# HGRN projections by seven block products: 12 of 16 row tiles of 28 pairs of weight tiles, with the weight sums on GpSimd

## The chip, the cores and the metric

The kernel runs on one core of a Trainium2 chip. The metric is the device time of one execution in microseconds (us), of which the median of several runs is given. TensorE is called PE here, its weight loads PEld, VectorE DVE, ScalarE ACT, GpSimd POOL, and the queue that starts most transfers SP.

## The reference, cut to what matters

Two layers are computed for 512 prompt tokens and 32 sample tokens (T = 544 columns): RWKV-7, then HGRN2. Everything is float32. The change is in the second layer:

```python
q, f_logit, i, z = jnp.split(x @ w_in, 4, axis=-1)       # x: (544, 2048), w_in: (2048, 8192)
f = lb + (1.0 - lb) * jax.nn.sigmoid(f_logit)
k = (1.0 - lb) * jax.nn.sigmoid(-f_logit)
q = jax.nn.silu(q) * HGRN_DK ** -0.5
...                                                      # per head: decays, scores A, states S, output o
o = o * lax.rsqrt(jnp.mean(o * o, axis=-1, keepdims=True) + NORM_EPS) * norm_w
out = (o.reshape(B, T, D) * jax.nn.silu(z)) @ w_o
```

There are 16 heads of 128 columns, so each head needs four output tiles of 128 columns of `x @ w_in`, each summed over 2048 rows of weights, in 16 row tiles of 128.

## The kernel before

Channels lie on the 128 partitions and the 544 tokens along the free dimension. One weight tile is 128x2048: 16 row tiles (kt = 0 to 15) for 128 output channels. A float32 product is made of three faster ones: ACT rounds the tile (`split_hi`, line 1757, into `w_hi`), DVE subtracts to get the rest (`split_lo`, line 1972, into `w_lo`), and `x` is split in the same way into `x_hi` and `x_lo`. For each row tile PE then does `w_hi*x_hi`, `w_hi*x_lo` and `w_lo*x_hi`, each for both halves of the tokens (TH = 272 columns): six matmuls a row tile, 96 a weight tile (`dense_kt`, line 129).

The tiles are numbered g: 0 to 15 are the output projection of the first layer, H0 = 16 to H1 - 1 = 79 the HGRN projections (four a head, in the order f, q, v, z), 80 to 95 the last projection. PE goes through them in order and accumulates even tiles in the two banks of `pair[0]`, odd ones in those of `pair[1]`. Weights are loaded by SP into `raw[g % 2]` (1 MB), once ACT and DVE have split the tile that lay there.

Into PE's stream of the projections of head e small matmuls are put by hand (`dense(g, steps)`), after a certain row tile: eight score levels (`level`), the transposes `v_by_token` and `k_by_token`, the state update `kv`, and of the head before it `late(e - 1)`: `outputs`, `sample_out`, `sample_state`, `norm`. ACT, DVE and POOL have their own hand-written order for each head:

- When tile f is done, DVE scales it by the token's norm (`scaled_out`, line 2036) into `F`; ACT makes both sigmoids (`sigmoids`, lines 1820 and 1821); DVE applies the bounds (`gate`).
- When tile q is done, DVE scales it into `qr`, ACT applies silu (line 1824), DVE multiplies by F (`first_q`). `level(e, 0)` needs the silu and the gated K, `level(e, 1)` the product, and `level(e, n)` from 2 on needs what `widen(e, n - 2)` on DVE made of K and Q.
- `out_copy`, `head_root` (two logarithms, an exponential, each kind with its own table load) and on DVE `finish` normalize and gate the output row of the head before, in place in `o`.
- POOL has two operations a head: `Sd = Ss * decay` (line 1957) and `Vm` (line 1962).

Between the layers, DVE and ACT make the 16 normalized rows of `x` one by one (`normed`, `high_part`, `low_part`), and PE runs tiles 16 and 17 together behind them (`two_dense`). Then tiles 18 and on follow as `dense`.

## Time and profile before

| | |
|---|---|
| runs | 2890.67, 2893.17, 2893.42 us; median 2893.17 us |
| profiled execution | span 2890.2 us from the first to the last instruction; no time of its own is listed |
| PE busy | 96% of the span |
| DVE, ACT, POOL busy | 46%, 39%, 4% |
| mean granted clock of PE | 0.988 of full speed |
| tiles 16 to 79 | from about 1656 us to about 2680 us |

The span is shorter than the median by 3.0 us, which lies outside the first and the last instruction. In the rows below, times without a unit are us from the start of the span, and the value behind `|` is the sum in us and the mean in ns of one.

### The profile page before, as it was taken

What the parts mean: (1) busy time and instruction counts of PE and PEld (TensorE: products, weight loads), DVE (VectorE), ACT (ScalarE), POOL (GpSimd) and SP (SyncE); (2) the same over time, 40 slices, a digit from 0 to 9 for tenths busy, and PEclk for the clock granted to TensorE, in tenths of its full rate; (3) what the DMA queues carried; (4) which work ended last, traced back from release to release, by engine and by line L of the source; (5) the groups of instructions that cost most, each with busy time, mean ns of one, the idle gap of its engine ahead of it and who ended that gap; (6) DMA issues with size and microseconds to landing.
All of it is one profiled execution on the core that took longest, in us unless ns stands there. A gap on an engine that the chain in (4) does not pass through costs nothing.

```text
span 2890.2 us, 81902 instructions
## 1 busy us (share of the span) xinstructions
PE 2779.4 (96%) x37320; PEld 2623.6 (91%) x37320; DVE 1337.4 (46%) x2213; ACT 1137.5 (39%) x1559; POOL 108.1 (4%) x92
## 2 busy tenths in 40 slices
PE   6999999999999999999889899999999999999997
PEld 5899999999998888887789889999999999999997
DVE  7334313313327778887632364344443434444324
ACT  5344323324415555555432353343333343234322
POOL 0000000000001111111000000000000000000000
PEclk8999999999999999999999999999999999999999
DMA  3333333334211111112132242223222222222323
GB/s 124 110 105 108 111 111 111 111 111 145 103 69 48 53 53 53 53 53 78 31 130 88 81 144 75 97 75 98 90 89 75 97 75 98 90 90 75 128 88 107
DMA packets 79639, 262.29 MB, mean 91 GB/s; under 512 B 15936, under 2 KB 25920, under 8 KB 58816
## 3 DMA queue, kind: packets, MB, share of 16 engines
q1 hardware_dynamic: 70080, 239.23, 24.6%
q10 hardware_dynamic: 9216, 17.83, 1.6%
q8 instruction: 295, 4.83, 0.7%
q14 instruction: 48, 0.39, 0.0%
HBM read 216.06 MB, written 40.97 MB: 89 GB/s over the span
## 4 chain that ended last, share of the span: by engine, by line
PE 48%; ACT 1%; DVE 1%; issue 0%; DVEq 0%; ACTq 0%
PE t_pair L129 40%; PE t_lev L1603 1%; PE t_tok L1666 1%; PE t_pair L139 1%; PE t_lev L1677 1%; PE t_tok L1684 1%; PE t_tok L1644 0%; PE t_lev L1654 0%; PE t_tok L1559 0%; PE t_lev L1656 0%; PE t_lev L1616 0%; PE t_tok L1627 0%; PE t_tok L1636 0%; DVE keep_o L2186 0%; PE t_lev L1611 0%
## 5 line engine op out<-in xcount | busy, mean ns | idle before, releaser
L129 PE MATMUL t_pair<-t_x_hi,keep_w_hi 128*128 128x272 f32 x3008 | 658.8, 300 | 17.9 <-DVE t_x_lo L1999 9.6
L129 PE MATMUL t_pair<-t_x_lo,keep_w_hi 128*128 128x272 f32 x3008 | 622.9, 288 | 0.0
L129 PE MATMUL t_pair<-t_x_hi,keep_w_lo 128*128 128x272 f32 x3008 | 622.2, 288 | 0.0
L129 PEld LDWEIGHTS t_pair<-t_x_hi,keep_w_hi 128*128 128x128 f32 x3008 | 468.8, 189 | 48.3 <-issue 25.9
L129 PEld LDWEIGHTS t_pair<-t_x_lo,keep_w_hi 128*128 128x128 f32 x3008 | 474.7, 189 | 0.0
L129 PEld LDWEIGHTS t_pair<-t_x_hi,keep_w_lo 128*128 128x128 f32 x3008 | 471.4, 188 | 0.0
L129 PE MATMUL w_pair<-a_x_hi,keep_w_hi 128*128 128x272 f32 x2016 | 428.0, 294 | 19.8 <-DVE a_x_lo L1052 19.0
L129 PE MATMUL w_pair<-a_x_lo,keep_w_hi 128*128 128x272 f32 x2016 | 419.1, 289 | 0.0
L129 PE MATMUL w_pair<-a_x_hi,keep_w_lo 128*128 128x272 f32 x2016 | 416.8, 288 | 0.0
L1038 DVE TENSOR_TENSOR keep_w_lo<-keep_raw,keep_w_hi 128x2048 fp32r<-128x2048 f32 x63 | 144.4, 2292 | 470.1 <-ACT keep_w_hi L791 470.1
L129 PEld LDWEIGHTS w_pair<-a_x_hi,keep_w_hi 128*128 128x128 f32 x2016 | 319.8, 189 | 26.4 <-issue 21.4
L129 PEld LDWEIGHTS w_pair<-a_x_lo,keep_w_hi 128*128 128x128 f32 x2016 | 317.4, 189 | 0.0
L129 PEld LDWEIGHTS w_pair<-a_x_hi,keep_w_lo 128*128 128x128 f32 x2016 | 317.3, 189 | 0.0
L1972 DVE TENSOR_TENSOR keep_w_lo<-keep_raw,keep_w_hi 128x2048 fp32r<-128x2048 f32 x94 | 215.5, 2293 | 218.2 <-ACT keep_w_hi L1757 218.2
L1757 ACT CAST keep_w_hi<-keep_raw 128x2048 fp32r<-128x2048 f32 x94 | 178.4, 1898 | 194.6 <-PE t_pair L129 194.6
L805 ACT ACTIVATE a_stage<-w_pair 128x544 f32<-128x544 f32 x64 | 40.0, 625 | 425.1 <-PE w_pair L129 425.1
L791 ACT CAST keep_w_hi<-keep_raw 128x2048 fp32r<-128x2048 f32 x63 | 120.2, 1908 | 31.0 <-ACT a_stage L805 28.0
L426 PEld LDWEIGHTS w_pair<-b_Ti,b_MT 64*64 64x64 f32 x2560 | 80.9, 135 | 29.1 <-DVE b_Ti L1073 28.2
L426 PE MATMUL w_pair<-b_Ti,b_MT 64*64 64x64 f32 x2560 | 91.5, 221 | 16.5 <-DVE b_Ti L1073 14.6
L2076 DVE TENSOR_TENSOR t_K<-t_K,t_E 128x256 f32<-128x256 f32 (+1 forms) x96 | 41.0, 427 | 139.3 <-PE t_lev L1603 52.4
L426 PE MATMUL w_pair<-b_TiT,b_X 64*64 64x64 f32 x2560 | 93.0, 222 | 0.9 <-issue 0.9
L426 PEld LDWEIGHTS w_pair<-b_TiT,b_X 64*64 64x64 f32 x2560 | 82.0, 136 | 10.3 <-DVE b_X L1062 5.3
(363 smaller groups left out, 3793.0 us busy)
## 6 DMA issues: line engine op xcount, KB each, us to landing
keep_raw<-in_w_in SPq DMA_DIRECT2D x64, 1024.0 KB, 4.9
keep_raw<-in_hgrn_in SPq DMA_DIRECT2D x64, 1024.0 KB, 4.9
keep_raw<-in_rwkv_wo SPq DMA_DIRECT2D x16, 1024.0 KB, 4.9
keep_raw<-in_hgrn_wo SPq DMA_DIRECT2D x16, 1024.0 KB, 4.9
t_Ss<-in_hgrn_s SPq DMA_DIRECT2D x16, 512.0 KB, 4.4
out_hgrn_s<-t_Sd SPq DMA_DIRECT2D x16, 512.0 KB, 6.8
scr_r<-a_stage ACTq DMA_DIRECT2D x16, 272.0 KB, 2.1
scr_k<-a_stage ACTq DMA_DIRECT2D x16, 272.0 KB, 2.1
```

The lines of the kernel that those rows point to most:

```text
L129: mm = pe.matmul(out[:, a, 0:TH], w, x[:, kt, a * TH:(a + 1) * TH], start=(kt == 0 and n == 0), stop=(kt == KT - 1 and n == 2))
L139: mm = pe.matmul(out, w, x[:, kt, cols], start=(kt == 0 and n == 0), stop=(kt == KT - 1 and n == 2))
L426: return pe.matmul(out[rows(o_half)], lhsT[rows(i_half)], rhs[rows(i_half)], start=start, stop=stop, skip_group_check=not (start and stop))
L791: act.copy(w_hi[2 if n == 2 else n % 2][:, :], raw[n % 2][:, :]).then_inc(p.raw_hi, 1)
L805: act.activation(halves(stage[n % 2][:, :]), pair[3 if n == 2 else n % 2][:, :, 0:TH], func).then_inc(p.evac, 1)
L1038: dve.tensor_tensor(w_lo[b][:, :], raw[n % 2][:, :], w_hi[b][:, :].bitcast(F32), ALU.subtract).then_inc(p.raw_lo, 1)
L1603: mm = pe.matmul(out[32 * q:32 * q + 32, 32 * c:32 * c + 32], K[:, cols], rhs[:, cols], start=True, stop=True)
L1666: mm = pe.matmul(sm_ps[:, DS * b:DS * b + DS], Ss[:, b, :], Q[:, SEQ + DS * b:SEQ + DS * b + DS], start=False, stop=(b == NB - 1), skip_gr ...
L1677: pe.matmul(out[:, :], ktok[r, 4, :], Vm[r, :, :].rearrange("p b v -> p (b v)"), start=True, stop=True).then_inc(s.sn_mm, 1)
L1757: act.copy(w_hi[g % 2][:, :], raw[g % 2][:, :]).then_inc(s.raw_hi, 1)
L1972: dve.tensor_tensor(w_lo[g % 2][:, :], raw[g % 2][:, :], w_hi[g % 2][:, :].bitcast(F32), ALU.subtract).then_inc(s.raw_lo, 1)
L2076: dve.tensor_tensor(kp[:, :, 0, :], kp[:, :, 0, :], ep[:, :, 1:2].broadcast_to([P, nb, m]), ALU.mult).then_inc(s.kx, 1)
```

## The change

The four tiles of each head from 1 to 14 are taken in two pairs: (f, q) and (v, z). This gives NQ = 28 pairs, q = 0 to 27. In a pair the 12 row tiles from 0 to 11 are done as a product of 2x2 blocks: two output tiles, row tiles even and odd, tokens of the first and the second half. Seven block products (`product(0)` to `product(6)`) of six steps, three matmuls a step, take the place of eight. Row tiles 12 to 15 are done plainly (`rest`, 16 steps). A pair has 58 steps, which is 174 matmuls of 272 columns, where two tiles had 192. Heads 0 and 15 keep their four plain tiles.

- **Weights.** The products need four sums of weight blocks (128x768); POOL makes them (`weight_sum_1` to `weight_sum_4`) from both raw tiles of the pair. Each of the seven operands is rounded by ACT (`item_hi`) and subtracted by DVE (`item_lo`) in pieces of 768 columns, in three slots that take turns; the plain rest of each tile in pieces of 512 (`rest_hi`, `rest_lo`).
- **Rows of x.** Sums of rows are made once, between tile 17 and tile 19: ACT scales twelve rows again (`scaled_rows`), DVE makes four sums for each pair of rows (`row_sums`), and both split them (`sums_hi`, `sums_lo`). They lie where `o` was, so they begin when all rows of `x1` are written to HBM. Six more sums take the place of parts of `x_hi` and `x_lo` behind tile 19 (`third_sum_hi`, `third_sum_lo`); what stood there goes to HBM and back (b12).
- **Results.** The blocks are put together from four banks: ACT copies a bank out (`first_out`, `second_out`, `third_out`), DVE adds the next (`upper_first`, `upper_fifth`, `upper_second`, `lower_second`, `lower_first`).
- **Gated rows** of heads 0 to 13 no longer fit in `o`: they are made in `acc`, written to HBM, and read back behind the last pair.
- Tile 76 (the first of head 15) is done with its even row tiles last.

The diff, cut to what the prediction speaks of:

```diff
+U = 6
+UW = U * P
+CW = D - 2 * UW
+ITEMS = 7
+KT_ORDER = [*range(0, 2 * U, 2), *range(1, 2 * U, 2), *range(2 * U, KT)]
+KT_PLACE = [KT_ORDER.index(kt) for kt in range(KT)]
...
+        To = Area(nc, "u6", keep.o_at).sb("To", [P, KT, 2, TH], F32R)
+        Tl = Area(nc, "u7", keep.lora_at).sb("Tl", [P, 2, 2, TH], F32R)
...
+        def item_slot(q, k):
+            return slot[3] if (q, k) == (NQ - 1, ITEMS - 1) else slot[(ITEMS * q + k) % 3]
+
+        def item_source(k):
+            return (raw[0][:, 0:UW], raw[0][:, UW:2 * UW], S2[:, :], S1[:, :], S3[:, :], S2[:, :], raw[1][:, UW:2 * UW])[k]
...
+            def next_weights(q):
+                for sem in (s.it_hi, s.it_lo):
+                    sp.wait_ge(sem, ITEMS * q + 2)
+                for sem in (s.c_hi, s.c_lo):
+                    sp.wait_ge(sem, 2 * q + 1)
+                for sem in (s.s2, s.s3, s.s4):
+                    sp.wait_ge(sem, q + 1)
+                sp.dma_start(raw[0][:, :], weight_tile(GS + 2 * q + 2)).then_inc(raw_in[0], 16)
+                for sem in (s.it_hi, s.it_lo):
+                    sp.wait_ge(sem, ITEMS * q + ITEMS)
+                for sem in (s.c_hi, s.c_lo):
+                    sp.wait_ge(sem, 2 * q + 2)
+                sp.wait_ge(s.s1, q + 1)
+                sp.dma_start(raw[1][:, :], weight_tile(GS + 2 * q + 3)).then_inc(raw_in[1], 16)
...
+            sp.wait_ge(s.hi, 2 * KT)
+            sp.wait_ge(s.lo, 2 * KT)
+            for n, t in enumerate((x_hi, x_lo)):
+                sp.dma_start(b12_kept(n), b12(t)).then_inc(s.b12_out, 16)
...
+            for e in range(1, KT - 1):
+                next_weights(2 * e - 2)
+                sp.wait_ge(s.sd, e)
+                sp.wait_ge(s.so_mm, e)
...
+                states(e - 1)
+                sp.wait_ge(s.yz, e)
+                sp.dma_start(d.yz[e - 1], acc[:, :]).then_inc(s.y_spill, 16)
+                next_weights(2 * e - 1)
...
+            sp.wait_ge(s.used, ITEMS * NQ)
+            sp.wait_ge(s.y_spill, 16 * SPILLED)
+            for e in range(SPILLED):
+                sp.dma_start(o[:, e, :], d.yz[e]).then_inc(s.y_back, 16)
+            weights(GE + 2)
...
+            def seven_products(q, steps):
+                X, Y, V = (banks[(q + i) % 3] for i in range(3))
...
+                def three_passes(out, hi, lo, n, x, start):
+                    w = slice(n * P, n * P + P)
+                    for m, (a, b) in enumerate(((hi[:, w], x[0]), (hi[:, w], x[1]), (lo[:, w], x[0]))):
+                        mm = pe.matmul(out, a, b, start=start and m == 0, stop=(m == 2), skip_group_check=True)
...
+                    if m in steps:
+                        steps[m]()
+
+                def product(k, out, start):
+                    pe.wait_ge(s.it_hi, ITEMS * q + k + 1)
+                    pe.wait_ge(s.it_lo, ITEMS * q + k + 1)
+                    hi, lo = item_slot(q, k)
+                    for j in range(U):
...
+                if q == 0:
+                    pe.wait_ge(s.evac, GS - 1)
+                    pe.wait_ge(s.t_lo, 2 * U)
+                else:
+                    pe.wait_ge(s.f0, q)
+                product(0, X, True)
+                if q:
+                    pe.wait_ge(s.g1, q)
+                product(1, Y, True)
+                pe.wait_ge(s.c_hi, 2 * q + 1)
+                pe.wait_ge(s.c_lo, 2 * q + 1)
+                rest(0, 0, Y, False, None)
+                if q == 0:
+                    pe.wait_ge(s.evac, GS)
+                else:
+                    pe.wait_ge(s.c12, q)
+                rest(0, 1, Z, True, s.c_used)
+                pe.wait_ge(s.p1, q + 1)
+                product(2, X, False)
...
+                product(4, X, False)
+                product(5, Z, False)
+                pe.wait_ge(s.c_hi, 2 * q + 2)
+                pe.wait_ge(s.c_lo, 2 * q + 2)
+                pe.wait_ge(s.up, q + 1)
+                rest(1, 1, V, False, s.v_ready)
+                pe.wait_ge(s.u3, q + 1)
+                product(6, X, False)
+                rest(1, 0, X, False, s.c_used)
...
+                keys = [lambda: k_by_token(e - 1), lambda: kv(e - 1)]
+                if 1 <= e < KT - 1:
+                    steps = dict(zip((10, 13, 15, 17, 19, 21, 24, 27), late(e - 1)))
+                    if e > 1:
+                        steps.update(zip((2, 6), keys))
...
+            def scaled_rows(j):
...
+            def sums_hi(j):
+                even, odd = ((K, Q), (v, zs))[j % 2]
+                act.wait_ge(s.t_sum, 4 * j + 4)
+                act.copy(T1[j][:, 0], even[:, half(0)]).then_inc(s.t_hi, 1)
+                act.copy(T42[j][:, :, 0], halves(odd[:, :])).then_inc(s.t_hi, 1)
+
+            def third_sum_hi(j):
+                act.wait_ge(s.b12_used, j + 1)
...
 
             def out_tile(q, g, post):
                 m = g % KT
...
+                out_copy(e - 1)
+                second_out(q, F)
+                item_hi(q, 5)
+                head_root(e - 1)
+                item_hi(q, 6)
+                rest_hi(q + 1, 0)
+                act.wait_ge(s.lev_mm, NLV * (e - 1) + 1)
+                third_out(q, qr)
+                item_hi(q + 1, 0)
+                sigmoids(e)
+                item_hi(q + 1, 1)
...
+                    for j in range(U - 2, U):
+                        scaled_rows(j)
+                        sums_hi(j - 1)
+                    sums_hi(U - 1)
...
+            def weight_sum_1(q):
+                pool.wait_ge(raw_in[1], 16 * ((GS + 2 * q) // 2))
+                if q:
+                    pool.wait_ge(s.it_hi, ITEMS * (q - 1) + 4)
+                    pool.wait_ge(s.it_lo, ITEMS * (q - 1) + 4)
+                pool.tensor_tensor(S1[:, :], raw[1][:, 0:UW], raw[1][:, UW:2 * UW], ALU.add).then_inc(s.s1, 1)
+
+            def weight_sum_2(q):
+                pool.wait_ge(raw_in[0], 16 * ((GS + 2 * q) // 2))
+                pool.wait_ge(s.s1, q + 1)
+                if q:
+                    pool.wait_ge(s.it_hi, ITEMS * (q - 1) + 6)
+                    pool.wait_ge(s.it_lo, ITEMS * (q - 1) + 6)
+                else:
+                    pool.wait_ge(s.tile_ready, GS)
+                pool.tensor_tensor(S2[:, :], S1[:, :], raw[0][:, 0:UW], ALU.subtract).then_inc(s.s2, 1)
+
+            def weight_sum_3(q):
+                if q:
+                    pool.wait_ge(s.it_hi, ITEMS * (q - 1) + 5)
+                    pool.wait_ge(s.it_lo, ITEMS * (q - 1) + 5)
+                pool.tensor_tensor(S3[:, :], raw[0][:, 0:UW], raw[1][:, 0:UW], ALU.subtract).then_inc(s.s3, 1)
...
+            def item_lo(q, k):
+                hi, lo = item_slot(q, k)
+                dve.wait_ge(s.it_hi, ITEMS * q + k + 1)
+                dve.tensor_tensor(lo[:, :], item_source(k), hi[:, :].bitcast(F32), ALU.subtract).then_inc(s.it_lo, 1)
...
+            def upper_first(q, t):
+                dve.wait_ge(s.p1, q + 1)
+                dve.wait_ge(s.c_used, 2 * q + 1)
+                dve.tensor_tensor(t[:, half(0)], banks[(q + 1) % 3], t[:, half(0)], ALU.add).then_inc(s.f0, 1)
...
+            def upper_second(q, t):
+                dve.wait_ge(s.up, q + 1)
+                dve.wait_ge(s.used, ITEMS * q + 6)
+                dve.tensor_tensor(t[:, half(1)], banks[3], t[:, half(1)], ALU.add).then_inc(s.c12, 1)
+                dve.wait_ge(s.f0, q + 1)
+                dve.wait_ge(s.c12, q + 1)
+                dve.tensor_tensor(t[:, :], t[:, :], rstd2[:, :], ALU.mult).then_inc(s.evac, 1)
+
+            def lower_second(q, t):
+                dve.wait_ge(s.u3, q + 1)
+                dve.wait_ge(s.v_ready, q + 1)
+                dve.tensor_tensor(t[:, half(1)], banks[(q + 2) % 3], t[:, half(1)], ALU.add).then_inc(s.g1, 1)
+                dve.wait_ge(s.g1, q + 1)
+                dve.tensor_tensor(t[:, half(1)], t[:, half(1)], rstd2[:, half(1)], ALU.mult).then_inc(s.q1s, 1)
+
+            def lower_first(q, t):
+                dve.wait_ge(s.c_used, 2 * q + 2)
+                dve.tensor_tensor(t[:, half(0)], banks[q % 3], rstd2[:, half(0)], ALU.mult).then_inc(s.evac, 1)
...
+            def row_sums(j):
+                even, odd = ((K, Q), (v, zs))[j % 2]
+                dve.wait_ge(s.t_in, 2 * j + 2)
+                dve.tensor_tensor(T3_raw[j], odd[:, half(1)], even[:, half(1)], ALU.subtract).then_inc(s.t_sum, 1)
+                dve.tensor_tensor(even[:, half(0)], even[:, half(1)], even[:, half(0)], ALU.subtract).then_inc(s.t_sum, 1)
+                dve.wait_ge(s.t_sum, 4 * j + 2)
+                dve.tensor_tensor(odd[:, half(1)], odd[:, half(1)], even[:, half(0)], ALU.subtract).then_inc(s.t_sum, 1)
+                dve.wait_ge(s.t_sum, 4 * j + 3)
+                dve.tensor_tensor(odd[:, half(0)], odd[:, half(0)], odd[:, half(1)], ALU.subtract).then_inc(s.t_sum, 1)
...
+            def sums_lo(j):
+                even, odd = ((K, Q), (v, zs))[j % 2]
+                dve.wait_ge(s.t_sum, 4 * j + 4)
+                dve.wait_ge(s.t_hi, 2 * j + 2)
...
+            row_sums(0)
+            for j in range(1, U - 2):
+                row_sums(j)
+                sums_lo(j - 1)
             split_lo(H0 + 2)
+            for j in range(U - 2, U):
+                row_sums(j)
+                sums_lo(j - 1)
+            sums_lo(U - 1)
...
+            def gates_pair(e, q):
+                if q:
+                    lower_first(q - 1, zs)
+                item_lo(q, 2)
+                item_lo(q, 3)
+                if e > 1:
+                    chain(e - 1)
+                item_lo(q, 4)
+                rest_lo(q, 1)
+                upper_first(q, F)
+                sample_states(e - 1)
+                item_lo(q, 5)
+                upper_fifth(q, F)
+                item_lo(q, 6)
+                finish(e - 1)
+                rest_lo(q + 1, 0)
+                item_lo(q + 1, 0)
+                upper_second(q, F)
+                item_lo(q + 1, 1)
+                lower_second(q, qr)
+                gate(e)
+
+            def values_pair(e, q):
+                lower_first(q - 1, qr)
+                item_lo(q, 2)
+                first_q(e)
+                item_lo(q, 3)
+                take(e, 0)
+                widen(e, 0)
+                rest_lo(q, 1)
+                item_lo(q, 4)
```

**DVE, the end of the (f, q) pair of a middle head.** Before, from the split of tile q to the first score mask (`keep_w_lo` is `split_lo`, L2045 to L2048 `gate`, L2120 and L2124 `finish`, L2056 `first_q`):

```order
L1972 TENSOR_TENSOR keep_w_lo0<-keep_raw0,keep_w_hi0 128x2048
L2045 TENSOR_SCALAR t_F<-t_F,t_oml,t_lb 128x544
L2046 TENSOR_SCALAR t_K<-t_K,t_oml 128x544
L2048 TENSOR_SCALAR t_F<-t_F 128x544
L2120 SCALAR_TENSOR_TENSOR keep_o<-keep_o,keep_params,t_rs 128x544
L2124 TENSOR_TENSOR keep_o<-keep_o,t_zs 128x544
L2036 TENSOR_TENSOR t_qr<-t_pair1,t_rstd2 128x544
L2056 TENSOR_TENSOR t_Q<-t_qr,t_F 128x544
```

After, from `item_lo(q, 6)` on (L2342 is `item_lo`, L2346 `rest_lo`, L2362 and L2365 `upper_second`, L2370 and L2372 `lower_second`, L2376 `lower_first`):

```order
L2342 TENSOR_TENSOR u1_it_lo_22007<-keep_raw1,u1_it_hi_22006 128x768
L2554 SCALAR_TENSOR_TENSOR t_acc<-t_acc,keep_params,t_rs 128x544
L2558 TENSOR_TENSOR t_acc<-t_acc,t_zs 128x544
L2346 TENSOR_TENSOR u2_c_lo_22014<-keep_raw0,u0_c_hi_22012 128x512
L2342 TENSOR_TENSOR u0_it_lo_22003<-keep_raw0,u0_it_hi_22002 128x768
L2362 TENSOR_TENSOR t_F<-t_pair1,t_F 128x272
L2365 TENSOR_TENSOR t_F<-t_F,t_rstd2 128x544
L2342 TENSOR_TENSOR u2_it_lo_22005<-keep_raw0,u2_it_hi_22004 128x768
L2370 TENSOR_TENSOR t_qr<-t_pair0,t_qr 128x272
L2372 TENSOR_TENSOR t_qr<-t_qr,t_rstd2 128x272
L2479 TENSOR_SCALAR t_F<-t_F,t_oml,t_lb 128x544
L2480 TENSOR_SCALAR t_K<-t_K,t_oml 128x544
```

`finish` has moved ahead of the scaling of F and of `gate`, and three splits for the next pair stand among them.

**POOL, a middle head.** Before, it has the two operations of lines 1957 and 1962 alone (now L2317 and L2325); after, eight sums stand around them (L2278, L2288, L2294, L2299 are `weight_sum_1` to `weight_sum_4`):

```order
L2294 TENSOR_TENSOR u3_wS3_22009<-keep_raw0,keep_raw1 128x768
L2299 TENSOR_TENSOR u3_wS2_22008<-keep_raw0,u3_wS2_22008 128x768
L2278 TENSOR_TENSOR t_wS1<-keep_raw1 128x768
L2288 TENSOR_TENSOR u3_wS2_22008<-t_wS1,keep_raw0 128x768
L2294 TENSOR_TENSOR u3_wS3_22009<-keep_raw0,keep_raw1 128x768
L2299 TENSOR_TENSOR u3_wS2_22008<-keep_raw0,u3_wS2_22008 128x768
L2317 TENSOR_TENSOR t_Sd<-t_Ss,t_E4 128x1024
L2278 TENSOR_TENSOR t_wS1<-keep_raw1 128x768
L2288 TENSOR_TENSOR u3_wS2_22008<-t_wS1,keep_raw0 128x768
L2325 TENSOR_TENSOR t_Vm<-t_vtok,t_k_h_seq 64x512
```

The third to fifth rows are the sums of the (v, z) pair that POOL starts as soon as the second raw tile of that pair has landed.

**ACT, between the last row of x and the split of tile 18.** Before (`t_F<-t_pair0` is the copy of tile 16, `keep_w_hi0` `split_hi` of tile 18):

```order
L1768 ACTIVATE t_rs<-keep_o 128x544
L1888 COPY t_F<-t_pair0 128x544
L1757 CAST keep_w_hi0<-keep_raw0 128x2048
L1781 ACTIVATE t_rstd2<-t_tok,keep_eps 128x544
L1784 ACT_TABLE_LOAD
L1784 ACTIVATE t_rstd2<-t_rstd2 128x544
```

After (L1984 is `scaled_rows`, L1989 and L1990 `sums_hi`):

```order
L2007 ACTIVATE t_rs<-keep_o 128x544
L1984 ACTIVATE t_K<-keep_o,keep_params 128x544
L1984 ACTIVATE t_Q<-keep_o,keep_params 128x544
L1984 ACTIVATE t_v<-keep_o,keep_params 128x544
L1984 ACTIVATE t_zs<-keep_o,keep_params 128x544
L1989 CAST u6_To_22016<-t_K 128x272
L1990 CAST u7_Tl_22017<-t_Q 128x2x272
...
L1990 CAST u6_To_22016<-t_Q 128x2x272
L2199 COPY t_F<-t_pair0 128x544
L1945 CAST keep_w_hi0<-keep_raw0 128x2048
```

Fourteen operations (eight scaled rows, three pairs of casts) now stand ahead of the copy and the split, and ten more between the split and the root of the norm (L1781 before).

## Rows read from the trace of the kernel before

**Rows 1.** The page: TensorE's busy time, share of the span, instructions.

```profile
PE 2779.4 (96%) x37320; PEld 2623.6 (91%) x37320; DVE 1337.4 (46%) x2213; ACT 1137.5 (39%) x1559; POOL 108.1 (4%) x92
```

**Rows 2.** Chain that ended last: start us, us, what (matmuls merged).

```profile
1480.36 163.70 PE t_pair L129 x1302
...
1999.01 3.22 PE t_pair L129 x24
2002.23 0.92 PE t_tok L1684 x4
...
2044.58 0.44 PE t_tok L1636 x4
...
2060.17 0.62 PE t_lev L1677
...
2061.22 3.22 PE t_pair L129 x24
...
2860.29 7.94 PE t_pair L139 x63
```

**Rows 3.** Windows: busy time of each engine over one head, then granted clock.

```profile
1999.00:2061.20 62.20, 62.20 (x673) 58.65 (x671) 25.64 (x50) 21.44 (x29) 2.93 (x2) 1.00 0.26 87
```

**Rows 4.** Groups by line and form on ACT and DVE.

```profile
L1757 ACT CAST keep_w_hi<-keep_raw 128x2048 fp32r<-128x2048 f32 x94 | 178.4, 1898 | 194.6 <-PE t_pair L129 194.6
L1820 ACT ACTIVATE t_K<-t_F 128x544 f32<-128x544 f32 x16 | 10.5, 658 | 0.2
L1871 ACT ACT_TABLE_LOAD x16 | 20.5, 1283 | 0.3
L1871 ACT ACTIVATE t_rs<-t_tok,keep_eps 128x272 f32<-128x272 f32 x32 | 13.9, 484 | 86.2 <-PE t_tok L1684 86.2
L1874 ACT ACTIVATE t_rs<-t_rs,keep_eps 128x544 f32<-128x544 f32 x16 | 12.0, 749 | 0.2
L1972 DVE TENSOR_TENSOR keep_w_lo<-keep_raw,keep_w_hi 128x2048 fp32r<-128x2048 f32 x94 | 215.5, 2293 | 218.2 <-ACT keep_w_hi L1757 218.2
L2036 DVE TENSOR_TENSOR t_v<-t_pair,t_rstd 128x544 f32<-128x544 f32 x16 | 11.5, 721 | 0.0
L2046 DVE TENSOR_SCALAR t_K<-t_K,t_oml 128x544 f32<-128x544 f32 x16 | 8.0, 497 | 0.0
L2186 DVE TENSOR_TENSOR keep_o<-keep_o,t_rstd 128x272 f32<-128x272 f32 x32 | 13.7, 433 | 13.2 <-ACT t_rstd L1945 13.2
```

**Rows 5.** Timeline of DVE: the second sample state sum of the same head.

```profile
2061.86 0.68 DVE L2115 TENSOR_TENSOR t_Sd<-t_tok,t_Sd 128x512 f32<-128x512 f32 x1
```

**Rows 6.** The raw weight tile, 1700 to 2680 us: its transfers.

```profile
DMA to landing us min/median/max: 4.8/4.9/6.3
```

**Rows 7.** POOL's operations by form, and a timeline of POOL and DVE in layer one.

```profile
L1957 POOL TENSOR_TENSOR t_Sd<-t_Ss,t_E 128x1024 f32<-128x1024 f32 x16 | 30.4, 1897 | 968.2 <-DVE t_E L2080 968.2
L1011 POOL TENSOR_TENSOR c_Vm<-b_toks,b_table 128x512 f32<-128x512 f32 x16 | 16.7, 1042 | 168.0 <-ACT b_toks L857 168.0
...
880.89 1.58 POOL L1014 TENSOR_TENSOR c_Um<-c_Us,b_table 128x512 f32<-128x512 f32 x1 [2.60 <-DVE c_Us L1077]
...
880.78 0.79 DVE L1110 SCALAR_TENSOR_TENSOR b_rk<-b_rt,keep_params,b_k 128x544 f32<-128x544 f32 x1
...
882.02 1.03 DVE L1115 TENSOR_TENSOR b_bb<-b_kkn,b_sga 128x544 f32<-128x544 f32 x1
```

**Rows 8.** Between the layers: DVE's timeline, PE's chain, a window (clock third last).

```profile
1695.09 0.78 DVE L1999 SCALAR_TENSOR_TENSOR t_x_lo<-keep_o,keep_params,t_x_hi 128x544 fp32r<-128x544 f32 x1 [2.52 <-ACT t_x_hi L1794]
1699.60 2.29 DVE L1972 TENSOR_TENSOR keep_w_lo<-keep_raw,keep_w_hi 128x2048 fp32r<-128x2048 f32 x1 [3.73 <-ACT keep_w_hi L1757]
...
1700.29 3.79 PE t_pair L129 x30
...
1714.40 0.43 PE t_lev L1603 x26
...
1655.00:1660.00 5.00, 1.37 (x6) 1.40 (x6) 4.24 (x8) 2.44 (x5) 0.00 (x0) 0.56 0.20 56
```

348 lines of the change are left out of this document (301 added, 47 removed).

## The prediction

> **What bounds the kernel now.** The page comes first: TensorE is busy in 96% of the span, the others in less than half of it [rows 1]. The chain of waits then tells whether that busy time is work. In the HGRN stage it runs through TensorE alone: 1302 matmuls in a row take 163.70 us, 0.1257 us each [rows 2]. From head to head the chain repeats after 2061.22 - 1999.01 = 62.21 us [rows 2], at full clock, with DVE busy in 25.6, ACT in 21.4 and POOL in 2.9 of it [rows 3]. Of the 62.21 us, 384 projection matmuls are 48.27; the other 13.94 are the small matmuls with the restart of the stream behind each. So a matmul taken out is worth 0.1257 us as long as PE has nothing to wait for, and the question is what the three other engines, with more work, make it wait for.
>
> **What is taken away.** A pair of tiles falls from 192 to 174 matmuls of the same shape, two pairs a head, 14 heads: 504 x 0.1257 = 63.4 us, 4.53 us a head. The new order writes one bank many times in succession; the half tiles at the end do so too and take 7.94 us for 63, 0.126 each [rows 2], so I count no loss. A head would take 57.68 us.
>
> **What the other engines get.** Durations on ACT and DVE grow with the columns. ACT: 544 columns 0.66, 2048 columns 1.90 us, so 768 take 0.84 and 512 take 0.63; DVE: 0.72 and 2.29, so 0.95 and 0.69, and 272 take 0.43 [rows 4]. A head now splits 14 pieces of 768 and 4 of 512 in place of 4 of 2048, which adds 6.7 us on ACT and 6.9 on DVE; the copies and additions from PSUM add some 2.4 and 3. Both stay below 36 of 57.7 us. POOL: 512 columns 1.04, 1024 columns 1.90 [rows 7], so a sum of 768 is an estimated 1.47 and eight are 11.8 us. No engine becomes the bound by its load; only the order in the queues can.
>
> **Where a queue is late.** Let 0 be the start of PE on a middle head's (f, q) pair; a step is three matmuls, 0.377 us. The late steps of the head before, from `k_by_token` to the norm's end, span 2061.22 + 3.22 + 0.92 - 2044.58 = 20.78 us with 102 projection matmuls in them, 12.82 us, so they cost 7.96; those ahead of the sample state cost 2060.17 - 2044.58 - 78 x 0.1257 = 5.79 [rows 2]. With 58 steps (21.87) the pair lasts 29.8 us.
>
> - The sample state is reached at 24 steps + 5.79 = 14.8. DVE has added both halves (2061.86 + 0.68) - 2060.17 = 2.4 us after its start [rows 2, 5], at 17.2; the norm stands only three steps behind (17.2) and may wait 0.1. It ends at 18.4.
> - ACT reads P2's bank at 17.0, casts item 5 and loads the logarithm's table (1.28) until 19.5. Two logarithms 0.9 (their starts overlap), a table 1.28, the exponential 0.75: 22.4. Cast of item 6: 23.2. DVE subtracts until 24.2. SP then starts the next raw tile, which lands 4.9 us later [rows 6]: 29.1.
> - DVE goes on with `finish` (0.78 + 0.73), 512 columns, 768 columns, an addition of 272, the scaling of F: 28.2. Sigmoids to 29.5, cast to 30.2, subtraction to 31.2, the addition and scaling of q to 32.0, the three operations of the gate (three times 0.50 [rows 4], less what they overlap: 1.3), `lower_first`: 33.7. Silu: 34.4.
> - PE starts the (v, z) pair at 29.85 and asks for the silu ten steps later, at 33.6 (`level(e, 0)`). It waits 0.8 us.
>
> The other handovers have room by the same sums: `kv` and the chain of states come within 0.1 us, the fourth product of the first pair has its operands 8 us early, and in the (v, z) pair each level comes 2.85 us after the one before, for which DVE needs 1.0 to 1.1 for `widen`, 0.95 for one split and 0.3 for a mask. Without anything else a head takes 57.7 + 0.1 + 0.8 = 58.6 us.
>
> **What POOL does to that.** At 29.1 the raw tile lands, in the middle of this chain, and POOL has three sums to do at once, until 33.5. The trace shows what that means. POOL's operation of 512 columns takes 1.04 us alone but 1.58 where it starts 0.11 us behind a DVE operation with two SBUF inputs; and the next such DVE operation, started while POOL runs, takes 1.03 instead of 0.72, while one with an input in PSUM between them runs as ever [rows 7]. So each keeps the other out for a whole operation. In the chain above, the subtraction, the scaling of q and perhaps the gate read SBUF only. The first sum ends at 30.7, the subtraction at 31.55, the second sum at 32.95; the scaling of q waits for it and ends at 33.3; gate, `lower_first` and silu end at 35.6. PE waits 2.0 us. The Trainium skill (GPSIMD Engine Reference, performance versus the Vector engine) gives 4.5 us for an addition of 2048 float32 columns on GpSimd; by it a sum would be about 1.7 us, and PE would wait 0.4 us more. No row here has that form.
>
> Whether the third sum then gets in ahead of the gate, the trace cannot tell: it would put 1.4 us on top. The gate's operations might not be kept out either. I take the value between, 2.0 us of waiting; ends 0.8 and 3.4. A head then takes 57.7 + 0.15 + 2.0 = 59.85 us, 2.36 less than before, 33 us in 14 heads.
>
> **The start of the layer.** Now the split of tile 18 ends at 1701.9 and the third level begins at 1714.40 [rows 8]. In the new order ACT and DVE pass the row sums back and forth from 1695.9 on, when the last `x_lo` is there [rows 8]. ACT: two scaled rows 1.4; DVE: four sums, of which three wait for the one before, 1.7, and the splits of the pair before, 1.1; then ACT may scale the next two. Eight rows take 12.2 us; copy of F and split of tile 18 end at 1712.9, where PE was free at 1704.08 (1700.29 + 3.79) [rows 8]. Four rows more, the root, sigmoids, gate, silu and the split of tile 19 end at 1731.5, and the third level begins at 1732.6: 18.2 us late. PE idles in two pieces of about 9 us. Between the layers, over 5 us in which it is busy in 1.4, its granted clock is 0.56 [rows 8], mostly the lower of its two levels (1.2 GHz of 2.4); after the second piece I put 2 us more for that. Together 20 us; nothing later gives them back, as PE is the chain from there on.
>
> **The end.** Tile 76 waits for `lower_first` (0.5), and its `outputs` come 6.4 us after its start while `chain` stands behind a split that ends at 7.4: 1.5 us. The read back of 14 rows (3.9 MB, 19 us at 1 MB in 4.9 us [rows 6]) has 30 us before tile 78. The rows' way out, 0.3 MB a head, is free. Together 2 us.
>
> **Sum.** -33 + 20 + 2 = -11 us on a span of 2890.2, whose runs stand at 2893.2 in the median: **2882 us**.
>
> **The rivals.**
>
> 1. *The port costs nothing at this place* (sums start after the gate, or only brush it): wait 0.8, a head 58.6, 3.6 x 14 = 50 less, -50 + 22 = -28: 2865 us. For it: the sums need only shift by two us, and nothing says how long they take. Against: rows 7. Chance 0.26.
> 2. *The forecast*, 2882 us, one sum in the way. Chance 0.32.
> 3. *The sums keep their place in line*, so that the third goes ahead of the gate: wait 3.4, a head 61.2, 14 us less, and 22 more for start and end: +8, 2901 us, slower. The change is slower as soon as PE waits over 4.53 - 22/14 = 3.0 us a head. For it: the third sum waits for nothing but the second, and POOL asked first. The Trainium skill (SBUF, the shared port between VectorE and GpSimd) says that the pair is held exclusively for a whole instruction, which starts first deciding, and counts also VectorE's faster modes among those that need it; the trace agrees for two SBUF inputs (1.58 for 1.04). Chance 0.26.
> 4. *POOL is slower still.* If the 1.58 us were its own price, a sum of 768 is 2.3 us; the second, from which item 2 of the (v, z) pair is cast, then ends past 34, and `item_lo(q, 2)` and `first_q` behind it are late too: 4.5 us or more a head, 2915 us. Chance 0.1. The rest, 0.06, is for stalls that I haven't seen, mostly upward.
>
> **Numbers.** About 0.2% (6 us) is what a measurement can tell here. Faster by more than that: rival 1, and all but the upper part of 2, 0.53; within: the upper part of 2 and the lower of 3, 0.17; slower 0.30. The range 2857 to 2911 reaches from beyond rival 1 to the middle between 3 and 4.
>
> **What would show it.** Right: PE with 504 fewer matmuls; heads 58.5 to 60.5 us apart; in the (v, z) pair the longest idle of PE ends with ACT's silu of `t_qr`; DVE's scaling of q mean above 0.6 us instead of 0.43; PE idle twice about 9 us between 1704 and 1733. Wrong: a head at 61 us or more; PE waiting in each pair for `it_lo` or for `widen`; sums on POOL near 2.3 us; or, on the other side, row sums that delay tile 18 by less than 5 us.

## The result, and the profile after

The changed kernel takes 2965.3 us (median of 4 runs, 2961.9 to 2968.6) against 2893.1 for the kernel before (2890.7 to 2893.4): ratio 1.025, 95% interval 1.023 to 1.026. It is slower by 72 us, where the forecast was 11 us faster, and lies above the range. The page, and then the waits of PE from the end of the first layer on (us in total, times, longest us):

```profile
span 2960.7 us, 82518 instructions
...
PE 2754.7 (93%) x36816; PEld 2586.5 (87%) x36816; DVE 1632.4 (55%) x2591; ACT 1258.3 (42%) x1869; POOL 337.5 (11%) x204
```

```profile
PE t_lev L1777 <- issue: 52.8, 14, 4.5
PE t_tok L1818 <- ACT t_ktok L2096: 17.2, 13, 1.6
PE t_pair L136 <- DVE keep_w_lo L2336: 9.0, 1, 9.0
PE t_lev L1777 <- ACT t_qr L2066: 7.2, 1, 7.2
```

PE has its 504 matmuls less (36816 for 37320), but its share of the span fell from 96% [rows 1] to 93%: 3.8 us a head are waited at the first score level (L1777, `level(e, 0)`), 1.3 before `kv` (L1818), and 16.2 once at the start of the layer. Where a wait is put down to "issue", the timeline below shows what PE waited for.

The transposes of v mark one head after the other. The first, the last and two in the middle, with the two stops between them:

```profile
1743.94 0.60 PE L1801 MATMUL t_tok<-t_k_ident,t_v 128*128 128x128 f32 x4
...
2012.26 0.60 PE L1801 MATMUL t_tok<-t_k_ident,t_v 128*128 128x128 f32 x4
...
2020.08 1.16 PE L1818 MATMUL t_tok<-t_vtok,t_ktok 128*128 128x128 f32 x8 [1.56 <-ACT t_ktok L2096]
...
2055.54 0.66 PE L1777 MATMUL t_lev<-t_qr,t_K 128*32 128x32 f32 x32 [3.70 <-issue]
...
2079.18 0.60 PE L1801 MATMUL t_tok<-t_k_ident,t_v 128*128 128x128 f32 x4
...
2727.82 0.60 PE L1801 MATMUL t_tok<-t_k_ident,t_v 128*128 128x128 f32 x4
```

Before, the same marks stood at 1724.22 and 2657.42. So the first head's is 19.7 us later; from the first to the last it is 983.9 us instead of 933.2, 50.7 more; from the last to the end of the span 232.9 instead of 232.8. 19.7 + 50.7 = 70.4, all of the 70.5 by which the span grew. Heads 1 to 14 are 65.95 us apart in the mean of 13, between 65.3 and 66.9, for 62.21 [rows 2] before.

The end of an (f, q) pair and the start of the (v, z) pair (its first matmul is the row at 2047.33), from the whole core's timeline:

```profile
2047.03 1.84 POOL L2278 TENSOR_TENSOR t_wS<-keep_raw 128x768 f32<-128x768 f32 x1 [25.49 <-DMA keep_raw<-in_hgrn_in]
2047.30 2.38 DVE L2342 TENSOR_TENSOR u_it_lo<-keep_raw,u_it_hi 128x768 fp32r<-128x768 f32 x1 [2.00 <-ACT u_it_hi L1957]
...
2047.33 0.29 PE L1657 MATMUL t_pair<-t_x_hi,u_it_hi 128*128 128x272 f32 x1
...
2049.00 2.38 POOL L2288 TENSOR_TENSOR u_wS<-t_wS,keep_raw 128x768 f32<-128x768 f32 x1
...
2049.61 0.43 DVE L2370 TENSOR_TENSOR t_qr<-t_pair,t_qr 128x272 f32<-128x272 f32 x1
2050.07 1.61 DVE L2372 TENSOR_TENSOR t_qr<-t_qr,t_rstd 128x272 f32<-128x272 f32 x1
...
2051.34 2.01 POOL L2294 TENSOR_TENSOR u_wS<-keep_raw 128x768 f32<-128x768 f32 x1
...
2051.60 2.04 DVE L2479 TENSOR_SCALAR t_F<-t_F,t_oml,t_lb 128x544 f32<-128x544 f32 x1
...
2052.26 1.28 ACT L2066 ACT_TABLE_LOAD   x1
...
2054.33 0.43 DVE L2376 TENSOR_TENSOR t_qr<-t_pair,t_rstd 128x272 f32<-128x272 f32 x1
...
2054.79 0.66 ACT L2066 ACTIVATE t_qr<-t_qr 128x544 f32<-128x544 f32 x1 [1.24 <-DVE t_qr L2376]
```

Read the ends. The first sum ends at 2048.87, the subtraction, started 0.27 behind it, at 2049.68: 2.38 us where it takes 0.95 alone. The second sum has been waiting and ends at 2051.38, and the scaling of q, which asks while it runs, at 2051.68 (1.61 for 0.44). The third ends at 2053.35, the gate's first operation at 2053.64 (2.04 for 0.56). Here POOL and DVE take turns, one whole instruction each; the addition with an operand in PSUM (L2370) goes through in 0.43 in the middle of a sum. The silu, for which PE waits, ends at 2055.45, 8.1 us into the (v, z) pair. The trace alone does not say whether PE's wait would be there without these turns, because the data of the sums come late.

TensorE's granted clock (the column PEclk, ahead of the DMA share) behind the stop at the first level:

```profile
2056.00:2058.00 2.00, 2.00 (x35) 1.69 (x30) 1.77 (x2) 0.45 (x1) 1.94 (x1) 0.50 0.04 8
...
2062.00:2064.00 2.00, 2.00 (x47) 1.81 (x47) 1.14 (x4) 0.00 (x0) 0.06 (x1) 1.00 0.09 37
```

After 3.7 us without work PE restarts at 0.50, its lower level, and is busy for some 6 us before it is back at the upper one. This head is one of the worse ones: over the ten us behind the first level the granted clock is 0.68 to 0.70 in four heads, 0.83 in nine, and 1.00 in head 1, where the stop lasted 3.16 us. In [rows 3] it was 1.00 throughout. The start of the layer:

```profile
1712.92 0.79 PE L136 MATMUL t_pair<-t_x_hi,keep_w_hi 128*128 128x272 f32 x2 [9.01 <-DVE keep_w_lo L2336]
...
1727.38 0.65 PE L1777 MATMUL t_lev<-t_qr,t_K 128*32 128x32 f32 x32 [7.21 <-ACT t_qr L2066]
...
1733.37 0.62 PE L1777 MATMUL t_lev<-t_Q,t_K 128*32 128x32 f32 x32
```

The third level begins 19.0 us after its place in [rows 8].

### The profile page after: what moved, and what is told of

It is laid out like the page before. It is cut to its first block, busy times and chain, and to the rows that moved or that the text cites. A ratio compares the mean times of both kernels' runs of the same rounds, so it can differ in the third digit from the quotient of the medians.

```text
span 2960.7 us, 82518 instructions
## 1 busy us (share of the span) xinstructions
PE 2754.7 (93%) x36816; PEld 2586.5 (87%) x36816; DVE 1632.4 (55%) x2591; ACT 1258.3 (42%) x1869; POOL 337.5 (11%) x204
## 4 chain that ended last, share of the span: by engine, by line
PE 35%; DVE 6%; issue 5%; ACT 5%; DMA 0%; POOL 0%; DVEq 0%; ACTq 0%; POOLq 0%
PE t_pair L136 15%; PE t_pair L1657 13%; PE t_lev L1777 1%; ACT u_it_hi L1957 1%; DVE t_F L2479 1%; PE t_pair L146 1%; PE t_tok L1840 1%; DVE t_qr L2372 1%; ACT L2113 1%; PE t_lev L1828 1%; PE t_tok L1818 1%; PE t_lev L1851 1%; DVE t_Q L2512 1%; DVE u_it_lo L2342 0%; DVE t_K L2510 0%
## 5 line engine op out<-in xcount | busy, mean ns | idle before, releaser
L1045 DVE TENSOR_TENSOR keep_w_lo<-keep_raw,keep_w_hi 128x2048 fp32r<-128x2048 f32 x63 | 144.4, 2292 | 469.9 <-ACT keep_w_hi L798 469.9
L136 PE MATMUL t_pair<-t_x_hi,keep_w_hi 128*128 128x272 f32 x1216 | 261.8, 297 | 27.6 <-DVE t_x_lo L2425 9.6
L136 PE MATMUL t_pair<-t_x_lo,keep_w_hi 128*128 128x272 f32 x1216 | 253.4, 290 | 0.0
L136 PE MATMUL t_pair<-t_x_hi,keep_w_lo 128*128 128x272 f32 x1216 | 253.1, 290 | 0.0
L136 PEld LDWEIGHTS t_pair<-t_x_hi,keep_w_hi 128*128 128x128 f32 x1216 | 192.2, 190 | 36.3 <-issue 19.9
L1657 PE MATMUL t_pair<-t_x_hi,u_it_hi 128*128 128x272 f32 x672 | 205.8, 306 | 2.0 <-DVE t_qr L2370 1.5
L1657 PE MATMUL t_pair<-t_x_hi,u_it_lo 128*128 128x272 f32 x672 | 196.3, 292 | 0.0
L1657 PE MATMUL t_pair<-t_x_lo,u_it_hi 128*128 128x272 f32 x672 | 196.2, 292 | 0.0
L136 PEld LDWEIGHTS t_pair<-t_x_lo,keep_w_hi 128*128 128x128 f32 x1216 | 194.0, 191 | 0.0
L136 PEld LDWEIGHTS t_pair<-t_x_hi,keep_w_lo 128*128 128x128 f32 x1216 | 192.3, 190 | 0.0
L2342 DVE TENSOR_TENSOR u_it_lo<-keep_raw,u_it_hi 128x768 fp32r<-128x768 f32 x84 | 104.5, 1246 | 79.8 <-ACT u_it_hi L1957 79.6
L2278 POOL TENSOR_TENSOR t_wS<-keep_raw 128x768 f32<-128x768 f32 x28 | 53.8, 1920 | 764.9 <-DMA keep_raw<-in_hgrn_in 764.9
```

Of the source, the lines that this page charges most:

```text
L136: mm = pe.matmul(out[:, a, 0:TH], w, x[:, kt, a * TH:(a + 1) * TH], start=(kt == order[0] and n == 0), stop=(kt == order[-1] and n == 2))
L1045: dve.tensor_tensor(w_lo[b][:, :], raw[n % 2][:, :], w_hi[b][:, :].bitcast(F32), ALU.subtract).then_inc(p.raw_lo, 1)
L1657: mm = pe.matmul(out, a, b, start=start and m == 0, stop=(m == 2), skip_group_check=True)
L2278: pool.tensor_tensor(S1[:, :], raw[1][:, 0:UW], raw[1][:, UW:2 * UW], ALU.add).then_inc(s.s1, 1)
L2342: dve.tensor_tensor(lo[:, :], item_source(k), hi[:, :].bitcast(F32), ALU.subtract).then_inc(s.it_lo, 1)
```

## Experiments

**Theory.** POOL's weight sums keep DVE out of SBUF for whole instructions, and the two waits of each head, with the low clock behind the first, follow from that. **Rivals:** the data of the sums or the raw tile come too late; or the queues' order is too tight by itself. For the start: the order of two queues, or the amount of work. Medians in us, with the ratio to the kernel before on the same chip:

| kernel | median | ratio, 95% interval |
|---|---|---|
| changed | 2965.3 | 1.023 to 1.026 |
| tiny_sums | 2868.8 | 0.990 to 0.993 |
| shadow | 2967.1 | 1.023 to 1.026 |
| third_late | 2951.8 | 1.019 to 1.022 |
| filler | 2945.3 | 1.017 to 1.020 |
| levels_late | 2952.5 | 1.020 to 1.023 |
| kcopy_levels | 2955.3 | 1.019 to 1.022 |
| sums_late | 2977.1 | 1.027 to 1.030 |
| order_only | 2908.1 | 1.005 to 1.009 |
| dve_sums | 2865.2 | 0.988 to 0.992 |
| rows_small | 2956.9 | 1.020 to 1.023 |
| start_order | 2952.1 | 1.019 to 1.022 |
| dve_sums_start | 2849.8 | 0.983 to 0.986 |

### Is it GpSimd, and is it the port? (tiny_sums, shadow)

```diff
+                w = 32 if q else UW
-                pool.tensor_tensor(S1[:, :], raw[1][:, 0:UW], raw[1][:, UW:2 * UW], ALU.add).then_inc(s.s1, 1)
+                pool.tensor_tensor(S1[:, 0:w], raw[1][:, 0:w], raw[1][:, UW:UW + w], ALU.add).then_inc(s.s1, 1)
```

and so for the other three sums: from the second pair on, 736 of the 768 columns of each sum are left out, and the results are not the reference's.

> Changed kernel, but from the second pair of tiles on GpSimd adds 32 of the 768 columns of each weight sum (the other columns are left as the first pair made them). Theory (GpSimd's sums keep VectorE out of SBUF at the end of each pair, and everything PE waits for follows from that): the wait of 3.7 us before the first level and the 1.3 us before `kv` shrink to under 1 us together, the granted clock stays at its upper level, a head takes 58 to 59 us instead of 66.0, and the kernel about 2965 - 14 x 7.3 = 2863 us. Rival (the raw tile lands too late and the ACT and DVE queues are too long by themselves, whatever GpSimd does): at least 2.5 of the 3.7 us stay, a head takes 64 us or more, 2937 us or more.

2868.8 us, a head 58.7. The same place in its timeline:

```profile
2082.00 0.96 DVE L2346 TENSOR_TENSOR u_it_lo<-keep_raw,u_it_hi 128x768 fp32r<-128x768 f32 x1 [2.00 <-ACT u_it_hi L1957]
...
2082.13 0.94 POOL L2290 TENSOR_TENSOR u_wS<-t_wS,keep_raw 128x32 f32<-128x32 f32 x1
...
2083.04 0.25 POOL L2297 TENSOR_TENSOR u_wS<-keep_raw 128x32 f32<-128x32 f32 x1
```

Each operation of DVE costs what it costs alone. And the lock is seen from the other side: 32 columns take POOL 0.25 us, but 0.94 when it starts 0.13 us behind the subtraction, until 0.11 us after that ends. This could still be the data, which come earlier too. shadow separates them:

```diff
+            def shadow(n):
+                for _ in range(n):
+                    pool.wait_ge(s.xs, shadows[0])
+                    pool.tensor_tensor(Sx[:, :], Sx[:, :], Sx[:, :], ALU.subtract).then_inc(s.xs, 1)
+                    shadows[0] += 1
...
                     weight_sum_3(q + 1)
+                    shadow(5)
                     weight_sum_4(q + 1)
+                    shadow(2)
```

> As tiny_sums (32 of 768 columns a sum from the second pair on), but GpSimd also executes, right behind the three sums that start together, five subtractions of 576 columns on a buffer that nobody else reads, and one to three behind the other sums, about as many columns in all as the sums had. So the data come as early as in tiny_sums and GpSimd is as busy as in the changed kernel. Theory (GpSimd's SBUF instructions keep VectorE's out, whatever they compute): VectorE's scaling of q and gate are slow again (over 1.2 us in the mean instead of 0.43 and 0.56), the waits before the first level and before `kv` are back, 2940 us or more. Rival (what was late in the changed kernel was the data of the sums, on which the casts at the head of ACT's queue wait): as tiny_sums, 2869 us, within 10.

`Sx` has 576 columns, 5 x 576 for the 3 x 768 of the sums, and 13 x 576 a head for 8 x 768. That is a quarter more columns in shorter instructions, so the equal time is in part chosen; what counts is that both waits return. The run takes 2967.1 us, as the changed kernel, with the data as early as in tiny_sums and the same columns left out. Groups of POOL and DVE (L2499 is the gate's first operation, L2392 the scaling of q), and PE's waits:

```profile
L2309 POOL TENSOR_TENSOR t_wSx<-t_wSx 128x576 f32<-128x576 f32 x176 | 228.1, 1296 | 8.7
```

```profile
L2499 DVE TENSOR_SCALAR t_F<-t_F,t_oml,t_lb 128x544 f32<-128x544 f32 x13 | 17.1, 1319 | 0.0
L2392 DVE TENSOR_TENSOR t_qr<-t_qr,t_rstd 128x272 f32<-128x272 f32 x13 | 14.6, 1127 | 0.5
```

```profile
PE t_lev L1778 <- issue: 50.2, 17, 4.2
PE t_tok L1819 <- ACT t_ktok L2097: 22.4, 13, 1.9
```

Sums on a buffer that nobody else reads make both waits as long as the real ones did. That is shown: it is POOL's occupation, not its results.

### What the turns and the clock are worth (third_late, filler)

```diff
+                    pool.wait_ge(s.f2, e + 1)
                     weight_sum_3(q + 1)
```

> Changed kernel, with the third of the three sums that GpSimd starts together held back until the gate is done. Theory (a waiting sum takes its turn ahead of the next VectorE operation): the gate no longer waits for the third sum, so the silu and the first level come 1.5 to 2 us earlier, the wait is about 2 instead of 3.7 us; 2965 - 14 x 1.7 = 2941 us if the clock still drops after it, 2905 us if it doesn't. Rival (the gate is slow for another reason, its own operations or the clock of something else): the gate's first operation keeps its mean of 1.86 us and the time stays within 5 us of 2965.

2951.8 us, 13.5 less for 24 expected. The gate's first operation is back at 0.55 us and the wait is 2.5 us. What is left of it: the scaling of q still takes 1.60 us, and the silu now stands behind the cast of item 2 and the table load on ACT, and that cast waits for the second sum. So ahead of the gate the third sum costs 1.2 us of the wait, not 1.7 to 2; and held back it blocks the subtraction after it (2.43 us for 0.95).

```diff
                 if n == 0:
+                    if 1 <= e < KT - 1:
+                        pe.wait_ge(s.o_ev, 2 * e)
+                        for _ in range(28):
+                            pe.matmul(out[:, 0:TH], x_hi[:, 0, 0:P], x_hi[:, 0, 0:TH], start=True, stop=True)
                     pe.wait_ge(s.kg, e + 1)
```

> Changed kernel plus 28 matmuls of 272 columns a head (28 x 0.126 = 3.5 us), results unused, on PE just ahead of its wait for the first level in heads 1 to 14. Theory (the half clock of some 6 us after that wait comes from PE's idling before it): the first level starts when it did, the granted clock stays at its upper level and a head is 2.7 us shorter: 2965 - 14 x 2.7 = 2927 us, with more work. Rival (the low clock comes with what follows, the small matmuls of the levels or the load of all engines together): the clock drops all the same, and the time is 2965 us or a little more.

2945.3 us: 20 us faster with 392 matmuls more. Its clock behind the first level:

```profile
2050.00:2052.00 2.00, 2.00 (x47) 1.81 (x47) 1.76 (x2) 1.41 (x3) 1.74 (x1) 1.00 0.03 8
```

The low clock comes from the idling, as expected; its price is 20 / 14 = 1.4 us a head, not 2.7, because only four heads are as slow as the one shown above. The changed kernel's own trace agrees: from the first level to the transposes of v a head takes 21.2 us at full clock (head 1, and the heads of filler), 22.5 to 22.6 where the ten us behind the level show 0.83, and 23.6 to 23.9 where they show some 0.70. That is 1.6 us in the mean of the heads.

### Can the order absorb it? (levels_late, kcopy_levels, sums_late, order_only)

```diff
-                    steps = {m: L(i) for i, m in enumerate((10, 12, 18, 24, 30, 36, 42, 48))}
-                    seven_products(2 * e - 1, {**steps, 53: lambda: v_by_token(e)})
+                    steps = {m: L(i) for i, m in enumerate((20, 22, 27, 32, 37, 42, 47, 52))}
+                    seven_products(2 * e - 1, {**steps, 55: lambda: v_by_token(e)})
```

> Changed kernel, with the eight levels of a head at steps 20, 22, 27, 32, 37, 42, 47, 52 of the (v, z) pair instead of 10 to 48, and `v_by_token` at 55 instead of 53; nothing is taken from GpSimd, ACT or DVE. Theory (the wait is only the lateness of the silu, 3.7 us = 10 steps, and the clock drop only follows it): both go, 3.7 + 2.7 us a head, the head is 59.5 to 60.5 us and the kernel about 2965 - 14 x 6.0 = 2881 us. Rival (VectorE has no slack behind it: the levels, then 5 steps = 2.5 us apart, wait for `widen`, and item 6 and the next raw tile come later by the same amount): the waits come back before levels 3 to 7 and `kv`, and the time is 2930 us or more.

2952.5 us: the rival. The wait at the first level is gone, and 38.7 us (3.0 a head) are waited before `kv` instead of 17.2. Next the copy of the keys was put ahead of the silu:

```diff
                 item_hi(q, 2)
                 if e > 1:
+                    k_copy(e - 1)
                     act.wait_ge(s.evac, H0 + 4 * e)
                     act.wait_ge(s.q1s, q)
                     silu(zs, s.zs)
-                    k_copy(e - 1)
```

> As levels_late, and in addition ACT copies the transposed keys (`k_copy`) ahead of the silu of `zs` instead of behind it. levels_late gave 2952.5 us, a head 64.7 us, with 2.9 to 3.7 us of waiting before `kv`. Theory (that wait is only the place of the copy behind a silu that waits for VectorE's blocked end of the pair): it goes, a head is 61.5 us, 2952 - 13 x 2.9 = 2914 us. Rival (VectorE itself is behind by then, so that the wait moves on to the chain of states or the item of the next product): more than half of it comes back at `outputs` or at the next product, 2935 us or more.

2955.3 us, the rival again. PE's waits of the two, levels_late first:

```profile
PE t_tok L1818 <- ACT t_ktok L2096: 38.7, 13, 3.7
```

```profile
PE t_lev L1828 <- DVE t_S L2538: 40.0, 14, 3.0
```

The same 3 us appear one instruction further on, at `outputs`, which waits for the chain of states on DVE. DVE is late in its own queue; what PE asks for first only decides where it shows. sums_late moved the three sums behind the gate:

```diff
+                    pool.wait_ge(s.f2, e + 1)
                     weight_sum_1(q + 1)
                     weight_sum_2(q + 1)
```

with the cast of item 2 behind the silu on ACT, its subtraction behind `first_q` on DVE.

> Changed kernel, sums still on GpSimd, but the three that start together wait until the gate is done; the cast of item 2 stands behind the silu on ACT and its subtraction behind `first_q` on VectorE. Theory (the price is VectorE's lost time, wherever the sums stand): the wait before the first level goes and the clock with it (5.3 us a head), but the three sums now block `first_q`, `widen` and the subtractions, item 2 is done past step 20, and PE waits 2 to 4 us for the third product or level 2: 2930 us, 2915 to 2950. Rival (only the place at the gate was bad, there is room behind it): all of the 5.3 us are kept, 2965 - 14 x 5.3 = 2891 us.

2977.1 us, worse than either and above the 2915 to 2950 of the theory. The first level has no wait left; the third pays for it:

```profile
2053.85 0.43 PE L1777 MATMUL t_lev<-t_qr,t_K 128*32 128x32 f32 x29 [0.21 <-issue]
...
2062.78 0.66 PE L1777 MATMUL t_lev<-t_Q,t_K 128*32 128x32 f32 x32 [4.57 <-DVE t_Q L2513]
```

The last kernel of this group has the order of dve_sums below, sums left on POOL (the diff is that one without its sums).

> Everything that dve_sums changed but its main point: the places of the casts, of the copy of the keys, of the chain of states and of the levels as there, and the weight sums on GpSimd where the changed kernel has them. dve_sums gave 2865 us. Theory (the gain of 100 us came from taking the sums off GpSimd): this stays near levels_late and third_late, 2940 to 2965 us, with waits of 3 us or more a head somewhere between the first level and the chain of states. Rival (the new order did it, and the sums could have stayed): within 25 us of dve_sums, 2890 us or less.

2908.1 us: my expectation (2940 or more) failed, and so did the rival's. The gate's first operation still takes 1.97 us in the mean and the wait at the first level is 2.3 us, but `kv` and `outputs` no longer wait in the middle heads. The clock falls behind about half of the stops only: 13 of the 14 last 2.2 to 2.3 us, and behind six of them the granted clock stays at 1.00, behind seven it falls. (The other lasts 3.1 us, and the clock falls.) One of each kind, and the two us that follow:

```profile
2037.79 0.43 PE L1777 MATMUL t_lev<-t_qr,t_K 128*32 128x32 f32 x29 [2.26 <-issue]
...
2284.38 0.43 PE L1777 MATMUL t_lev<-t_qr,t_K 128*32 128x32 f32 x29 [2.25 <-issue]
```

```profile
2039.00:2041.00 2.00, 2.00 (x47) 1.82 (x46) 2.00 (x7) 1.69 (x3) 1.16 (x1) 1.00 0.00 0
...
2286.00:2288.00 2.00, 2.00 (x37) 1.94 (x28) 2.00 (x4) 1.27 (x3) 1.58 (x1) 0.50 0.00 0
```

So on the way from the changed kernel to dve_sums, 100 us faster, the better order is worth 57 us while the sums are on POOL, and the change of engine then the other 43. The split holds for this way only: tiny_sums, in the old order, is already 96 us faster. It is POOL's sums that make the order dear. No run has the full sums on DVE in the old order.

### The sums on the other engine (dve_sums)

```diff
                     lower_first(q - 1, zs)
-                item_lo(q, 2)
-                item_lo(q, 3)
+                weight_sum_1(q)
+                weight_sum_2(q)
+                weight_sum_3(q)
                 if e > 1:
                     chain(e - 1)
+                item_lo(q, 2)
+                weight_sum_4(q)
+                item_lo(q, 3)
...
                 lower_first(q - 1, qr)
-                item_lo(q, 2)
+                weight_sum_1(q)
                 first_q(e)
+                weight_sum_2(q)
+                weight_sum_3(q)
+                item_lo(q, 2)
+                take(e, 0)
+                widen(e, 0)
                 item_lo(q, 3)
-                take(e, 0)
-                widen(e, 0)
+                weight_sum_4(q)
```

On ACT `k_copy` goes ahead of the silu of `zs`, and `item_hi(q, 2)` behind both silus; on PE the levels stand at steps 14 to 49 in place of 10 to 48.

> Changed kernel with all weight sums on VectorE (eight of 768 columns a head, 0.95 us each, 7.6 us more for it, 44 of some 59 us in all), nothing on GpSimd; the sums stand behind `lower_first` and before the chain of states or the masks; the cast of item 2 stands behind the silu; the copy of the keys ahead of it; levels at steps 14, 16, 24, 29, 34, 39, 44, 49. Theory (it was the shared port and GpSimd's slowness, not the amount of elementwise work): a head takes 58.5 to 60 us, and the kernel 2965 - 13.5 x 6.7 = 2875 us, faster than before by 0.6%. Rival (with the sums on it VectorE's queue is too long at the handovers): waits of over 3 us a head before item 2's product or the third level, 2910 us or more.

2865.2 us, 1.0% faster than before, a head 58.7 us. DVE's sum and gate, and PE's waits:

```profile
L2323 DVE TENSOR_TENSOR u_wS<-t_wS,keep_raw 128x768 f32<-128x768 f32 x26 | 24.8, 955 | 1.2
...
L2466 DVE TENSOR_SCALAR t_F<-t_F,t_oml,t_lb 128x544 f32<-128x544 f32 x14 | 7.8, 557 | 0.0
```

```profile
PE t_pair L136 <- DVE keep_w_lo L2295: 9.0, 1, 9.0
PE t_lev L1777 <- issue: 8.2, 28, 0.4
PE t_lev L1777 <- ACT t_qr L2066: 6.9, 1, 6.9
```

With 7.6 us of sums more, DVE is on time in all middle heads (PE waits 0.4 us at most). A sum takes 0.955 us for 1.9 to 2.3 on POOL and delays nothing but what stands behind it.

### The start (rows_small, start_order, dve_sums_start)

In rows_small only the first row sum is computed in full; the others work on 8 and 16 columns, and all six places use the first one's rows, so the results are not the reference's:

```diff
-                for kt, t in ((2 * j, even), (2 * j + 1, odd)):
-                    act.activation(t[:, :], o[:, kt, :], ACT.Copy, scale=par(params, "pre1", kt)).then_inc(s.t_in, 1)
+                w = 16 if j else T
+                for kt, t in ((2 * j, even), (2 * j + 1, odd)):
+                    act.activation(t[:, 0:w], o[:, kt, 0:w], ACT.Copy, scale=par(params, "pre1", kt)).then_inc(s.t_in, 1)
```

> Changed kernel, but of the six row sums at the start of the layer only the first is computed in full, and all six places use it; the other five are operations of 8 to 16 columns in the same order. Nothing later changes. Theory (the ping-pong of ACT and DVE over wide rows costs the start 20 us): the wait of 9.0 us before tile 18 and most of the 7.2 us before the first level go, and with them the low clock behind them; about 2965 - 16 = 2949 us. Rival (the start would be as late anyway, behind the root and the sigmoids): less than 5 us, 2960 or more.

2956.9 us, 8.4 less for 16 expected. Waits of 4.2 us before tile 18, 2.0 before the first level and 1.5 before the third stay. The first mark (the transposes of v of head 0) comes 12.3 us earlier, at 1731.6, but 2.8 of these are lost again up to head 1's, whose first level is followed by the lower clock here and was not in the changed kernel. start_order keeps the work and changes its place, with the later sums in buffers that head 0 doesn't use:

```diff
             row_sums(0)
-            for j in range(1, U - 2):
-                row_sums(j)
-                sums_lo(j - 1)
+            row_sums(1)
             split_lo(H0 + 2)
-            for j in range(U - 2, U):
-                row_sums(j)
-                sums_lo(j - 1)
-            sums_lo(U - 1)
+            sums_lo(0)
+            sums_lo(1)
...
                 widen(e, 4)
                 take(e, 5)
                 widen(e, 5)
+                if e == 0:
+                    row_sums(4)
+                    sums_lo(3)
                 widen(e, 6)
```

and so for rows 2, 3 and 5 and on ACT.

> Changed kernel with the start of the layer in another order and the same work: two row sums, then at once the split of tile 18, root, sigmoids, gate, silu and the split of tile 19; the other four row sums, on buffers that head 0 doesn't use (`acc`, `sq`, `rs`, `zs`), lie between the masks of head 0 under tiles 18 and 19. Theory (the 20 us of the start are the order of two queues, not the amount of work; rows_small, with a sixth of the work in the old order, took off only 8.4 us): both waits at the start fall to under 1.5 us together and no low clock follows them, 2965 - 18 = 2947 us. Rival (the row sums are too much for VectorE and ACT wherever they stand): PE waits for them later, at levels 4 to 7 of head 0 or before the first pair, and 2957 us or more.

2952.1 us, 13.2 less. Its marks:

```profile
1709.47 0.43 PE L1780 MATMUL t_lev<-t_qr,t_K 128*32 128x32 f32 x29 [1.05 <-ACT t_qr L2069]
...
1724.34 0.60 PE L1804 MATMUL t_tok<-t_k_ident,t_v 128*128 128x128 f32 x4
1729.48 0.45 PE L1788 MATMUL t_lev<-t_Q,t_K 128*32 128x32 f32 x16 [1.75 <-DVE t_K L2516]
...
1742.60 0.36 PE L1660 MATMUL t_pair<-t_x_hi,u_it_hi 128*128 128x272 f32 x1 [2.15 <-issue]
```

PE waits 1.05 us at the first level, and then 1.75, 0.65 (the transposes of K at 1736.10) and 2.15, 4.6 in all, under tile 19 and before the first pair: 5.6 of the 20 stay, and the time agrees (19.7 - 13.2 = 6.5). So two thirds of the start's cost were the place of the row sums; the rest is work that ACT and DVE still do on the path. rows_small doesn't contradict this: to take five sixths of the work out of the bad place helps about as much as to move it.

> dve_sums (2865 us) with the start of start_order. If the two costs are independent, one in the heads and one ahead of them, the gains add: 2865 - 18 = 2847 us, ratio 0.984 to the kernel before. If GpSimd's sums had a part in the start, it is less than what start_order gains by itself.

2849.8 us, 15.4 below dve_sums; the gains add, to within a few us. This version is 1.5% faster than the kernel before (ratio 0.985, 0.983 to 0.986).

## Why the prediction was wrong, point by point

- **The matmuls taken out: right.** 504 fewer. Without the port a head was to take 58.6 us; tiny_sums has 58.7, and its 2868.8 us stand beside rival 1's 2865.
- **The start: right in size.** 20 forecast, 19.7 measured, with stops of 9.0 and 7.2 us and the third level at 1733.4 for 1732.6. But it was put down to the row sums' work; with all the work kept and moved, 13.2 of the 20 us go.
- **The port: the mechanism right, the price wrong.** This is the first step that failed: "I take the value between, 2.0 us of waiting", built on a sum of 1.47 us of which one stood in the way. A sum takes 1.82 us undisturbed (0.25 us for 32 columns) and 2.33 where it waits its turn. The 1.47 was drawn from two rows, 1.04 and 1.90 us, whose operations repeat one operand along an axis (`broadcast_to`), while a sum reads two full ones; shadow's 576 columns, one buffer twice, take 1.14 undisturbed, which does fit those rows. (No run compares the two forms at one width.) All three sums stood in the way; the subtraction, the scaling and the gate lost 1.4, 1.2 and 1.5 us. The silu ended 8.1 us into the (v, z) pair where my sum had 35.6 - 29.85 = 5.75, and the wait was 3.7 us. It took rival 3 (the third sum ahead of the gate) together with a good part of rival 4 (sums of 2.3 us), which I had priced as alternatives. The Trainium skill (SBUF — State Buffer, who interferes with whom) says that the pair is held for a whole instruction by whichever starts first, that a `tensor_scalar` can enter a mode that needs it, and that an instruction of DVE outside such modes with at most one input in SBUF does not contend; the trace agrees on all three (2.38 for 0.95 at L2342, 2.04 for 0.56 at L2479, 0.43 at L2370). I had named that rule and given it 0.26.
- **`kv`: not foreseen, the second step that failed.** "The other handovers have room by the same sums" was worked out without the port. At the end of the (v, z) pair the next sums keep `widen` waiting, and between two of them stands POOL's old operation `Vm` (L2325):

```profile
2014.17 1.22 POOL L2325 TENSOR_TENSOR t_Vm<-t_vtok,t_k_h_seq 64x512 f32<-64x512 f32 x1
...
2014.41 3.04 DVE L2512 TENSOR_TENSOR t_Q<-t_Q,t_E 128x256 f32<-128x256 f32 x1
2015.35 1.82 POOL L2294 TENSOR_TENSOR u_wS<-keep_raw 128x768 f32<-128x768 f32 x1
...
2018.74 0.66 ACT L2066 ACTIVATE t_zs<-t_zs 128x544 f32<-128x544 f32 x1 [3.66 <-DVE t_zs L2376]
2019.30 0.57 ACT L2095 COPY t_ktok<-t_tok 128x512 f32<-128x512 f32 x1
```

  0.42 us became 3.04, the silu and the copy behind it followed, and PE waited 1.3 us in each head. Note that POOL had two turns in a row here, `Vm` until 2015.39 and a sum until 2017.17, while DVE's instruction had asked since 2014.41. It is so in all 13 heads with a `kv` wait (3.04 us each time); why DVE was passed over there and not at the gate, no run shows.
- **The clock: not foreseen in the heads.** I had put 2 us on it at the start, where PE stops for 9 us, and nothing on the stop that I forecast in every head. filler prices it at 1.4 us a head. In order_only, whose stops are near the 2.0 us forecast, it fell behind seven of 13 and cost 0.4 us a time in the mean (heads of 62.0 to 62.4 us for 61.5 to 62.0 at 1.00), so the term would have been small had the wait been right.
- **The end: right.** Tile 76 waits 0.62 us and its `outputs` 1.08, 1.7 for the 2 us forecast; the kernel before has neither stop. They lie ahead of the last mark, within the 50.7 us; behind it nothing is lost (232.9 for 232.8), so the rows read back cost nothing.

A head took 65.95 us for 59.85, and from the first mark to the last PE took 50.7 us more, where the forecast for the heads was 33 less. tiny_sums shows where the 7.2 us a head over its own 58.7 lie, since it gives PE the same matmuls in the same order. In the head whose v marks are 1946.57 and 2012.26, PE falls behind tiny_sums by 1.4 us at `kv`, 0.6 before the second product of the (v, z) pair (which waits for L2370), 3.6 at the first level and 1.4 in the matmuls at the lower clock, 6.9 in all. The head after the next, from 2079.18, has 1.3, 0.3, 3.6 and 1.4. Four heads lose 2.5 instead of 1.4 by the clock. Nothing of size is left over; against all of this the forecast's term for the port was 1.25 us (58.6 to 59.85).

## What to carry to other kernels

Before elementwise work is given to an idle GpSimd, look at what VectorE does in the same microseconds: each instruction there with two SBUF inputs, or a `tensor_scalar` on SBUF alone, may have to wait for GpSimd's, so the price to expect is one whole GpSimd instruction for each VectorE instruction on the path, and it was two at `widen`. Here 7.6 us a head were cheaper on VectorE, which is busy 566 of 800 us with them (dve_sums_start, 1800 to 2600), than 16.3 us on GpSimd (228.6 us in 14 heads), which had hardly anything else to do. When a wait is moved and comes back at the next handover in the same size, the queue behind it is late as a whole; take work out of it, or reorder it from its start. And a PE stop is to be priced with the clock behind it.

## What was new about the hardware

- A GpSimd addition of 32 columns: 0.25 us alone, 0.94 started 0.13 us behind a VectorE subtraction with two SBUF inputs. The lock held GpSimd out as it does VectorE, here although GpSimd's instruction was the shorter one by far.
- Where instructions of both engines waited, they mostly alternated, also in shadow: while its five GpSimd instructions run in a row, VectorE's get through one after each. But at `widen` GpSimd took two turns in a row in each of 13 heads (3.04 us for 0.42).
- A stop of PE of some 2.25 us can go either way with the clock: in order_only 1.00 throughout behind six such stops, 0.50 behind seven. The stops of 3.7 us and more in the changed kernel were all followed by 0.50 (13 of 13), the one of 3.16 us by 1.00. 28 matmuls without use in the longer stops made the kernel 20 us faster.
